# Sampled tokens' expert halves over one and a half passes, their row broadcasts on ScalarE's queue

## The chip, the cores and the metric

The kernel runs on one core of a Trainium2 chip. The time is device microseconds of one execution, first to last instruction with what lies around them. Before the change: median 3320.12 us of three runs (3313.13, 3320.12, 4272.85).

## What is computed

One decoding layer for 256 prompt tokens (with 16 meta tokens ahead) and 32 sampled tokens (8 sequences of 4), all in float32: an input projection, an RWKV-7 mixer and a sparse attention side by side, an output projection, a layer norm, and a retrieval of experts ("PEER"), then the last layer norm. The change concerns the experts:

```python
q = (xf @ wq).reshape(n, PEER_HEADS, 2, PEER_HALF)          # 8 heads
s = jnp.einsum('nhpd,hpkd->nhpk', q, subkeys)               # 2 x 128 keys
# top 16 of each half, top 16 of their sums: 8 x 16 = 128 experts a token, of 128 x 128
h = gelu(einsum('nd,nhkd->nhk', xb, u_tab[eb]))             # row of U against the token
y = einsum('nhk,nhkd->nd', gb * h, v_tab[eb])               # gate * h times row of V
```

U and V have 16,384 rows of 2048 values each.

## The kernel before

**Prompt tokens, all experts.** The 256 prompt tokens (ND) are multiplied by the whole of U and V, and a gate that is zero for experts not chosen does the selecting. `peer_experts` walks a list of 288 weight tiles of 1 MB, `tiles`, each [128, 2048]: 16 "o" (output projection), 16 "q" (queries), with 32 "u" tiles between them, then 32 more "u" of the first half of the experts (half 0), the value pass of half 0 ("v", tiles 96 to 159, `v_zero` = 96), the U pass of half 1 (tiles 160 to 223, `u_one` = 160) and the value pass of half 1 (224 to 287, `v_one` = 224). A value pass is two sweeps of 32 tiles, one for each half of the output columns.

**One tile's way.** SP loads it into one of four buffers once the tile four before it is used. ScalarE rounds it to float32r (`raise_tile`, L2050), waiting for the load and for the tile two before to be used. VectorE subtracts to get the low part (`lower_tile`, L2393). TensorE forms three products of high and low parts (`split_product`, L254 to L256), 48 matmuls a tile. For a "v" tile the gates of two experts are split likewise: ScalarE in L2086, VectorE in L2400. For a "u" tile ScalarE applies Gelu on the way out (`curve`, L2112 and L2116) and VectorE multiplies by gates (`weigh`, L2602). Every engine has one loop over the tiles; in its turn t ScalarE rounds tile t + 2 and VectorE lowers tile t + 2 before the other work of turn t. Each engine works in the order written.

**Gates of half 1.** They are kept in DRAM (`g_rest`), 32 steps of 8 tokens. In the U pass of half 1 Pool reads step k back into one of three buffers `rest` for tile 160 + k; ScalarE (`spread_gates`, L2130) and VectorE (`times`, L2615) use it, and Pool waits for both of step k - 3.

**Sampled tokens, chosen experts only.** For each of the 32 sampled tokens 128 rows of U are gathered, one a partition, in two halves of 1024 columns, so 64 halves n. Buffers `u_row` and `u_x` exist twice. For half n:

- Pool waits for the sum of half n - 2, broadcasts the token's half row from DRAM (`x_rows`) to all partitions of `u_x` (L2014) and gathers the rows with an indirect DMA into `u_row` (L2016), both counted on `u_in`;
- VectorE multiplies them in turn v_zero + n (`times_x`, L2557), after `lower_tile` and `lower_gates` of that turn;
- ScalarE sums along the row in the turn after (`sum_products`, L2134).

So a half is due at every tile of the value pass of half 0. Then the sums are joined (`join_halves`, turn 161), Gelu is applied, and from tile 165 on every second tile TensorE forms one token's value rows (`own_values`, L2274), 32 in all, in bank 7. Pool gathers them (L2027) into `v_row`, two buffers in the same place as `u_row` and `u_x`; the reads of `g_rest` stand between the gathers on its queue. `y_rows` is copied out in turn `v_one` + 5, turned back and added to the sampled tokens' columns, which the second sweep of half 1's values (from tile 256) waits for.

Of the kernel before, what the change touches and what calls it, by code (L numbers as in the profile page):

```python
# [19 lines left out]
P = 128  # L20
# [5 lines left out]
TS = B * S  # L26
# [1754 lines left out]
HALF = D // 2  # L1781
G8 = 8
ND = NY - TS
STEPS = ND // G8
# [52 lines left out]
def peer_experts(cx, a, xT, ident, x_rest, gb, ones, high, low, g_rest, x_rows):  # L1837
# [8 lines left out]
    with ExitStack() as st:  # L1846
# [23 lines left out]
        u_row, u_x = [lay("u_row0", [P, HALF])], [lay("u_x0", [P, HALF])]  # L1870
# [4 lines left out]
        rest = [sb(f"rest{s}", [P, EH, G8]) for s in range(3)]  # L1875
# [35 lines left out]
        for p in pair:  # L1911
# [21 lines left out]
        weighed, g_raised, g_lowered = cx.sem("px_weighed"), cx.sem("px_g_high"), cx.sem("px_g_low")  # L1933
        x_turned, x_taken, x_stored, listed = (cx.sem(f"px_{x}") for x in ("x_turned", "x_taken", "x_stored", "listed"))
        u_in, v_in = ([cx.sem(f"px_{x}{k}") for k in range(2)] for x in ("u_in", "v_in"))
        u_timed, u_summed, u_joined, u_curved, v_ready, v_used = (cx.sem(f"px_{x}") for x in (
            "u_timed", "u_summed", "u_joined", "u_curved", "v_ready", "v_used"))
        y_kept, y_turned, y_added = (cx.sem(f"px_{x}") for x in ("y_kept", "y_turned", "y_added"))
        v_zero, u_one, v_one = tile_of["v", 0, 0, 0], tile_of["u", 1, 0], tile_of["v", 1, 0, 0]
        FIRST_V = 5  # L1940
        finished, drained, link = cx.sem("px_finished"), cx.sem("px_drained"), cx.sem("px_link")

        early = [t for t, x in enumerate(tiles) if x[0] != "v"]
# [14 lines left out]
        def step_number(hf, k):  # L1958
            return hf * STEPS + k
# [6 lines left out]
        with cx.block() as block:  # L1966
# [30 lines left out]
            @block.gpsimd  # L1997
            def _(pool):
                pool.wait_ge(x_taken, 4)
                pool.dma_start(x_rows, xrows).then_inc(x_stored, 16)  # L2000
                for k in range(STEPS):
                    pool.wait_ge(rest_copied, k + 1)
                    pool.dma_start(g_rest[k], rest[k % 3][:].rearrange("p e t -> p (e t)")) \
                        .then_inc(rest_stored[k % 3], 16)

                halves = a["peer_u_rows"].rearrange("e (h d) -> (e h) d", h=2)
                pool.wait_ge(x_stored, 16)
                pool.wait_ge(listed, 3)
                pool.wait_ge(placed, STEPS)
                for n in range(2 * TS):  # L2010
                    if n >= 2:
                        pool.wait_ge(u_summed, n - 1)
                    part_ = x_rows[n // 2:n // 2 + 1, n % 2 * HALF:n % 2 * HALF + HALF]
                    pool.dma_start(u_x[n % 2], bass.AP(part_.tensor, part_.offset, [[0, P], [1, HALF]])) \  # L2014
                        .then_inc(u_in[n % 2], 16)
                    pool.indirect_dma_start(u_row[n % 2], None, halves, bass.IndirectOffsetOnAxis(  # L2016
                        ids[:, 1 + n % 2, n // 2:n // 2 + 1], 0)).then_inc(u_in[n % 2], 16)

                for s in range(3):
                    pool.wait_ge(rest_stored[s], 16 * len(range(s, STEPS, 3)))  # L2020

                def fetch_values(j):
                    if j < 2:
                        pool.wait_ge(u_summed, 2 * TS)
                    else:
                        pool.wait_ge(v_used, j - 1)
                    pool.indirect_dma_start(v_row[j % 2], None, a["peer_v"], bass.IndirectOffsetOnAxis(  # L2027
                        ids[:, 0, j:j + 1], 0)).then_inc(v_in[j % 2], 16)

                for k in range(STEPS):  # L2030
                    if k >= 3:
                        pool.wait_ge(timed, step_number(1, k - 3) + 1)
                        pool.wait_ge(spread, step_number(1, k - 3) + 1)
                    pool.dma_start(rest[k % 3][:].rearrange("p e t -> p (e t)"), g_rest[k]) \
                        .then_inc(rest_loaded[k % 3], 16)
                    if k >= 3 and k % 2:
                        fetch_values((k - 3) // 2)
                for j in range((STEPS - 2) // 2, TS):
                    fetch_values(j)

            def from_pair(k):
# [3 lines left out]
            def _(act):  # L2045
# [73 lines left out]
                def spread_gates(hf, k):  # L2119
# [9 lines left out]
                        src = rest[k % 3][:]  # L2129
                    act.activation(gates[:, n:EH, k * G8:k * G8 + G8], src[:, n:EH, :], ACT.Copy).then_inc(spread, 1)  # L2130

                def sum_products(n):
                    act.wait_ge(u_timed, n + 1)
                    act.activation(u_row[n % 2], u_row[n % 2], ACT.Copy,  # L2134
                                   accum_out=acts[:, n // 2, n % 2:n % 2 + 1]).then_inc(u_summed, 1)

                for k in range(4):
                    raise_x(k)
# [2 lines left out]
                for t, x in enumerate(tiles):  # L2141
                    if x[0] == "o" and t:
                        square_chunk(t - 1)
                    if t == KT - 1:
                        square_chunk(KT - 1)
                    if t + 2 < NT:
                        raise_tile(t + 2)
                        if tiles[t + 2][0] == "v":
                            raise_gates(t + 2)
                    if t == KT - 1:  # L2150
                        root()
                        for k in range(4):
                            bend(k)
                    if x[0] == "q":
                        take_query(t)
                    elif x[0] == "u":
                        curve(t)
                    if t and tiles[t - 1][0] == "q":
                        copy_score(tiles[t - 1][1])
                    head, r = divmod(t + 1 - KT, PER_HEAD)  # L2160
                    if r == 4 and 1 <= head <= PH:
                        act.wait_ge(diffed, head)
                        act.activation(diff[:], diff[:], ACT.Exp).then_inc(exped, 1)
                    for hf, k in after[t]:
                        spread_gates(hf, k)
                    if 0 <= t - 1 - v_zero < 2 * TS:
                        sum_products(t - 1 - v_zero)
                    if t == u_one + 2:
                        act.wait_ge(u_joined, 1)
                        act.activation(own[:], own[:], ACT.Gelu).then_inc(u_curved, 1)  # L2170
                    if t == v_one + 5:
                        act.wait_ge(v_used, TS)
                        act.activation(y_rows, bank[7][:], ACT.Copy).then_inc(y_kept, 1)

            @block.tensor
            def _(pe):
# [107 lines left out]
                for t, x in enumerate(tiles):  # L2284
                    if x[0] == "v":
                        down(t)
                    else:
                        product(t)
                    if t == 1:
                        shift_sum()  # L2290
                    if t == KT - 1:
                        norm_sums()
                    if 1 <= t - KT <= 4:
                        turn_rows(t - KT - 1)
                    j, odd = divmod(t - u_one - FIRST_V, 2)
                    if 0 <= j < TS and not odd:
                        own_values(j)
                    if t == v_one + 6:
                        turn_back()
                    if t and tiles[t - 1][0] == "q":  # L2300
                        score_chunk(tiles[t - 1][1])
                    if t == place_first - 1:
                        turn()
                    for hf, k in after[t]:
                        if hf == 0:
                            place(k)

            @block.vector
            def _(v):
# [243 lines left out]
                    v.tensor_copy(xrows[:, 512 * r:512 * r + 512], bank[7][0:TS, :]).then_inc(x_taken, 1)  # L2553

                def times_x(n):
                    v.wait_ge(u_in[n % 2], 32 * (n // 2 + 1))
                    v.tensor_tensor(u_row[n % 2], u_row[n % 2], u_x[n % 2], ALU.mult).then_inc(u_timed, 1)  # L2557

                def join_halves():
# [7 lines left out]
                def own_column(j):  # L2567
                    if j >= 2:
                        v.wait_ge(v_used, j - 1)
                    v.tensor_scalar(column[j % 2][:], iota[:, 0:TS], float(j), own[:, j:j + 1], ALU.is_equal,  # L2570
                                    ALU.mult).then_inc(v_ready, 1)
# [52 lines left out]
                for t, x in enumerate(tiles):  # L2624
# [21 lines left out]
                        lower_x(3, 1)  # L2646
                    if 1 <= t - KT <= 4:
                        take_rows(t - KT - 1)
                    if 0 <= t - v_zero < 2 * TS:
                        times_x(t - v_zero)  # L2650
                    if t == u_one + 1:
                        join_halves()
                    if t == u_one + 3:
                        spread_own()
                    j, odd = divmod(t + 1 - u_one - FIRST_V, 2)
                    if 0 <= j < TS and not odd:
                        own_column(j)
                    if t == v_one + 7:
                        add_own()
                    if 0 <= t - KT < PER_HEAD * PH + 5:  # L2660
                        select(t - KT)
# [150 lines left out]
```

## Time and profile before

| | us |
|---|---|
| median of three runs | 3320.12 |
| profiled execution | 3312.37 |
| its span, first to last instruction | 3310.7 |
| TensorE busy in the span | 2949.3 (89%) |
| VectorE busy | 1935.5 (58%) |
| ScalarE busy | 1094.9 (33%) |
| Pool busy | 248.4 (8%) |

The profile is that of one execution. "Busy" for TensorE counts overlapped matmuls once. DMA issuing is not counted as busy on an engine; the instruction is shown with the time it held the issuing queue. "Landing" is from a DMA's issue to its last byte. A wait is idle time of an engine just before an instruction, with the instruction or DMA that ended it. The granted clock is a share of TensorE's 2.4 GHz.

### The profile page before, as it was taken

To read this page: it belongs to the slowest core of one execution; us is meant where nothing else is said; L and a number is where in the kernel's file an instruction comes from. 1 tells how busy PE (TensorE), PEld (TensorE's weight loads), DVE (VectorE), ACT (ScalarE), POOL (GpSimd) and SP (SyncE) were. 2 spreads that over 40 slices of the span, in tenths; PEclk is the share of its full clock that TensorE was granted. 3 is DMA by queue.
4 is the path that set the end of the run, shared out by engine and by line. 5 is a ranking of instruction groups with operands and counts; after the bars stand their busy time and mean duration, and the time that the engine had idled before them with its cause. 6 is when DMAs were issued, how large, how long until landed. Compare 5 with 4: busy or idle time off the path is not lost. (4 is left out here: it accounts for less than half of the span.)

```text
span 3310.7 us, 52455 instructions
## 1 busy us (share of the span) xinstructions
PE 2949.3 (89%) x21558; PEld 2652.6 (80%) x21558; DVE 1935.5 (58%) x3399; ACT 1094.9 (33%) x1333; POOL 248.4 (8%) x357
## 2 busy tenths in 40 slices
PE   3999947999985687798999999999999999999995
PEld 2999916878762233497999999999999999999995
DVE  3444336666646763266999989666664444444554
ACT  1222211211112110134444433555554433344441
POOL 0000000000003101100000000232231100000000
PEclk7999957998986557898999999999999999999998
DMA  2444300000015403463555454899998777755551
GB/s 113 152 156 160 112 29 11 17 11 21 11 38 136 153 2 113 146 217 119 182 172 171 168 179 172 307 341 338 332 330 297 286 271 250 253 177 180 182 187 55
DMA packets 145613, 541.86 MB, mean 164 GB/s; under 512 B 25226, under 2 KB 45427, under 8 KB 114387
## 3 DMA queue, kind: packets, MB, share of 16 engines
q1 hardware_dynamic: 110018, 400.11, 35.3%
q0 software_dynamic: 35376, 138.70, 11.9%
q8 instruction: 154, 2.52, 0.3%
q14 instruction: 65, 0.52, 0.0%
HBM read 521.85 MB, written 16.80 MB: 163 GB/s over the span
## 5 line engine op out<-in xcount | busy, mean ns | idle before, releaser
L2393 DVE TENSOR_TENSOR px_w_r<-px_w,px_wh 128x2048 fp32r<-128x2048 f32 x287 | 657.1, 2290 | 461.1 <-ACT px_wh L2050 457.5
L2050 ACT ACTIVATE px_wh<-px_w 128x2048 fp32r<-128x2048 f32 x287 | 549.7, 1915 | 960.6 <-PE px_bank L256 784.9
L254 PE MATMUL px_bank<-pe_high,px_wh 128*128 128x256 f32 (+1 forms) x2560 | 737.1, 288 | 29.2 <-DVE pe_low L2319 14.4
L255 PE MATMUL px_bank<-pe_low,px_wh 128*128 128x256 f32 (+1 forms) x2560 | 733.7, 287 | 0.0
L256 PE MATMUL px_bank<-pe_high,px_w_r 128*128 128x256 f32 (+1 forms) x2560 | 729.3, 285 | 0.0
L254 PEld LDWEIGHTS px_bank<-pe_high,px_wh 128*128 128x128 f32 x2560 | 487.9, 191 | 58.2 <-issue 37.6
L255 PEld LDWEIGHTS px_bank<-pe_low,px_wh 128*128 128x128 f32 x2560 | 486.9, 190 | 0.0
L256 PEld LDWEIGHTS px_bank<-pe_high,px_w_r 128*128 128x128 f32 x2560 | 484.5, 189 | 0.0
L254 PE MATMUL px_pair<-px_arena_gh,px_wh 128*128 128x256 f32 x1024 | 291.5, 285 | 15.5 <-DVE px_arena_gl L2400 15.5
L254 PE MATMUL px_bank<-px_arena_gh,px_wh 128*128 128x256 f32 x1024 | 290.8, 284 | 7.4 <-DVE px_arena_gl L2400 7.2
L255 PE MATMUL px_pair<-px_arena_gl,px_wh 128*128 128x256 f32 x1024 | 290.3, 284 | 0.0
L256 PE MATMUL px_pair<-px_arena_gh,px_w_r 128*128 128x256 f32 x1024 | 290.2, 283 | 0.0
L255 PE MATMUL px_bank<-px_arena_gl,px_wh 128*128 128x256 f32 x1024 | 289.7, 283 | 0.0
L256 PE MATMUL px_bank<-px_arena_gh,px_w_r 128*128 128x256 f32 x1024 | 289.7, 283 | 0.0
L254 PE MATMUL in_acc<-mixT_r,in_wh 128*128 128x304 f32 x784 | 238.4, 304 | 40.5 <-DVE in_w_r L314 40.5
L256 PE MATMUL in_acc<-mixT_r,in_w_r 128*128 128x304 f32 x784 | 238.9, 305 | 0.0
L255 PE MATMUL in_acc<-x_inT_r,in_wh 128*128 128x304 f32 x784 | 237.1, 302 | 0.0
L254 PEld LDWEIGHTS px_pair<-px_arena_gh,px_wh 128*128 128x128 f32 x1024 | 197.1, 192 | 17.9 <-DVE px_w_r L2393 16.9
L254 PEld LDWEIGHTS px_bank<-px_arena_gh,px_wh 128*128 128x128 f32 x1024 | 196.5, 192 | 11.4 <-DVE px_w_r L2393 8.0
L255 PEld LDWEIGHTS px_pair<-px_arena_gl,px_wh 128*128 128x128 f32 x1024 | 197.2, 193 | 0.0
L256 PEld LDWEIGHTS px_pair<-px_arena_gh,px_w_r 128*128 128x128 f32 x1024 | 197.1, 192 | 0.0
L255 PEld LDWEIGHTS px_bank<-px_arena_gl,px_wh 128*128 128x128 f32 x1024 | 196.5, 192 | 0.0
(469 smaller groups left out, 4688.4 us busy)
## 6 DMA issues: line engine op xcount, KB each, us to landing
px_w<-in_peer_u SPq DMA_DIRECT2D x128, 1024.0 KB, 4.9
px_w<-in_peer_v SPq DMA_DIRECT2D x128, 1024.0 KB, 5.8
in_w<-in_w_in SPq DMA_DIRECT2D x49, 1024.0 KB, 4.9
px_w<-in_peer_wq SPq DMA_DIRECT2D x16, 1024.0 KB, 5.0
px_lay_u_x<-x_rows POOLq DMA_DIRECT2D x32, 512.0 KB, 5.9
px_arena_u_x<-x_rows POOLq DMA_DIRECT2D x32, 512.0 KB, 6.0
px_w<-in_w_o SPq DMA_DIRECT2D x15, 1024.0 KB, 5.0
pq_pages<-in_kv_pages SPq DMA_DIRECT2D x48, 256.0 KB, 6.9
```

Of the source, the lines that this page charges most:

```text
L254: pe.matmul(out, w_high, high, start=start, stop=False, skip_group_check=True)
L255: pe.matmul(out, w_high, low, start=False, stop=False, skip_group_check=True)
L256: return pe.matmul(out, w_low, high, start=False, stop=stop, skip_group_check=True)
L2050: act.activation(w_high[t % 2][:], w[t % SL][:], ACT.Copy).then_inc(raised, 1)
L2393: v.tensor_tensor(w_low[t % SL][:], w[t % SL][:], w_high[t % 2][:], ALU.subtract) \
```

## The change

- The 64 halves are no longer due at every tile of one pass. `half_at` gives the tile of each: halves 0 to 47 at tiles 96 + 4n // 3 (96, 97, 98, 100, 101, 102, 104, ...: three of every four tiles), halves 48 to 63 at every second tile from 160 on (160, 162, ... 190).
- The broadcast of the token's half row leaves Pool's queue. ScalarE issues it (`fetch_x`), for half n + 2 right after it has summed half n, and for halves 0 and 1 two tiles ahead of the value pass. It has semaphores of its own, `u_x_in`, and `times_x` waits for both.
- Pool's queue mixes the gathers of halves with the reads of `g_rest`: all reads up to step T - 160 stand before the gather for tile T. The gathers of value rows come after all of them.
- Joining, Gelu and spreading move to tiles 193 to 195. Value rows are used at tiles 198 + 5j // 3 (198, 199, 201, 203, 204, ... 249) instead of every second tile from 165; copying out, turning back and adding move to tiles 250, 251 and 252 (before: 229 to 231).

The diff, cut to its core:

```diff
-        FIRST_V = 5
+        half_at = {v_zero + 4 * n // 3 if n < 48 else u_one + 2 * (n - 48): n for n in range(2 * TS)}
+        joined_at = u_one + 33
+        value_at = {joined_at + 5 + 5 * j // 3: j for j in range(TS)}
+        kept_at = max(value_at) + 1
...
-                for n in range(2 * TS):
+                def fetch_half(n):
                     if n >= 2:
                         pool.wait_ge(u_summed, n - 1)
-                    part_ = x_rows[n // 2:n // 2 + 1, n % 2 * HALF:n % 2 * HALF + HALF]
-                    pool.dma_start(u_x[n % 2], bass.AP(part_.tensor, part_.offset, [[0, P], [1, HALF]])) \
-                        .then_inc(u_in[n % 2], 16)
                     pool.indirect_dma_start(u_row[n % 2], None, halves, bass.IndirectOffsetOnAxis(
                         ids[:, 1 + n % 2, n // 2:n // 2 + 1], 0)).then_inc(u_in[n % 2], 16)
...
+                def fetch_rest(k):
+                    if k >= 3:
+                        pool.wait_ge(timed, step_number(1, k - 3) + 1)
+                        pool.wait_ge(spread, step_number(1, k - 3) + 1)
+                    else:
+                        pool.wait_ge(rest_stored[k], 16 * len(range(k, STEPS, 3)))
+                    pool.dma_start(rest[k % 3][:].rearrange("p e t -> p (e t)"), g_rest[k]) \
+                        .then_inc(rest_loaded[k % 3], 16)
...
+                k = 0
+                for t, n in half_at.items():
+                    while k < STEPS and k <= t - u_one:
+                        fetch_rest(k)
+                        k += 1
+                    fetch_half(n)
+                for k in range(k, STEPS):
+                    fetch_rest(k)
+                for j in range(TS):
                     fetch_values(j)
...
+                def fetch_x(n):
+                    part_ = x_rows[n // 2:n // 2 + 1, n % 2 * HALF:n % 2 * HALF + HALF]
+                    act.dma_start(u_x[n % 2], bass.AP(part_.tensor, part_.offset, [[0, P], [1, HALF]])) \
+                        .then_inc(u_x_in[n % 2], 16)
+
                 def sum_products(n):
                     act.wait_ge(u_timed, n + 1)
                     act.activation(u_row[n % 2], u_row[n % 2], ACT.Copy,
                                    accum_out=acts[:, n // 2, n % 2:n % 2 + 1]).then_inc(u_summed, 1)
+                    if n + 2 < 2 * TS:
+                        fetch_x(n + 2)
...
+                    if t == v_zero - 2:
+                        act.wait_ge(x_stored, 16)
+                        act.wait_ge(placed, STEPS)
+                        fetch_x(0)
+                        fetch_x(1)
+                    if t - 1 in half_at:
+                        sum_products(half_at[t - 1])
...
                 def times_x(n):
-                    v.wait_ge(u_in[n % 2], 32 * (n // 2 + 1))
+                    v.wait_ge(u_in[n % 2], 16 * (n // 2 + 1))
+                    v.wait_ge(u_x_in[n % 2], 16 * (n // 2 + 1))
...
-                    if 0 <= t - v_zero < 2 * TS:
-                        times_x(t - v_zero)
-                    if t == u_one + 1:
+                    if t in half_at:
+                        times_x(half_at[t])
+                    if t == joined_at:
                         join_halves()
```

## Rows read from the trace of the kernel before

**Rows 1.** Stretches: length, busy us of PE, PEld, DVE, ACT, POOL; clock, DMA share, GB/s.
```profile
2080.00:2480.00 400.00, 377.12 (x3092) 373.19 (x3091) 261.14 (x201) 224.40 (x254) 109.37 (x124) 1.00 0.92 333
2480.00:2513.00 33.00, 30.19 (x243) 29.99 (x242) 16.42 (x21) 15.28 (x21) 5.77 (x9) 0.95 0.81 296
2513.00:2700.00 187.00, 187.00 (x1547) 172.35 (x1546) 83.56 (x106) 78.33 (x116) 28.97 (x41) 1.00 0.79 289
2935.00:3240.00 305.00, 305.00 (x2544) 305.00 (x2544) 156.74 (x118) 129.16 (x106) 0.00 (x0) 1.00 0.56 183
```

**Rows 2.** Instructions on the weight tiles, 2940 to 3240 us: durations, first and last start.
```profile
L2393 DVE TENSOR_TENSOR px_w_r<-px_w,px_wh x52: 2291/2292/2293, 2943.0 to 3236.8; 128x2048 fp32r<-128x2048 f32 x52
...
DMA to landing us min/median/max: 4.9/5.0/6.3
```

**Rows 3.** The same view, 2079 to 2500 us.
```profile
L2393 DVE TENSOR_TENSOR px_w_r<-px_w,px_wh x68: 2277/2285/2294, 2079.9 to 2499.4; 128x2048 fp32r<-128x2048 f32 x68
L1993 SPq DMA_DIRECT2D px_w<-in_peer_v x61: 367/368/368, 2083.6 to 2455.7; - x61
...
DMA to landing us min/median/max: 5.0/8.3/10.8
```

**Rows 4.** TensorE's waits, 2080 to 2494 us: us in total, times, longest.
```profile
PE px_pair L254 <- DVE px_arena_gl L2400: 15.5, 13, 2.3
PE px_bank L254 <- DVE px_arena_gl L2400: 7.2, 7, 1.6
PE px_bank L254 <- DVE px_w_r L2393: 2.8, 1, 2.8
```

**Rows 5.** VectorE's waits in the same stretch.
```profile
DVE px_lay_u_row L2557 <- DMA px_lay_u_row<-in_peer_u_rows,px_ids: 68.5, 22, 5.6
DVE px_arena_u_row L2557 <- DMA px_arena_u_row<-in_peer_u_rows,px_ids: 50.5, 20, 4.8
```

**Rows 6.** Timeline (start us, us) of one unstalled tile, last value pass: ScalarE, VectorE, TensorE.
```profile
2998.69 1.92 ACT L2050 ACTIVATE px_wh<-px_w 128x2048 fp32r<-128x2048 f32 x1 [3.32 <-PE px_bank L256]
3000.51 0.61 ACT L2086 ACTIVATE px_arena_gh<-px_gates 128x512 fp32r<-128x512 f32 x1
...
3000.64 2.29 DVE L2393 TENSOR_TENSOR px_w_r<-px_w,px_wh 128x2048 fp32r<-128x2048 f32 x1 [2.87 <-ACT px_wh L2050]
3002.85 0.68 DVE L2400 TENSOR_TENSOR px_arena_gl<-px_gates,px_arena_gh 128x512 fp32r<-128x512 f32 x1
...
3004.19 0.28 PE L254 MATMUL px_bank<-px_arena_gh,px_wh 128*128 128x256 f32 x1
```

**Rows 7.** Timeline of one half in the first value pass: VectorE, ScalarE, Pool.
```profile
2347.06 0.68 DVE L2400 TENSOR_TENSOR px_arena_gl<-px_gates,px_arena_gh 128x512 fp32r<-128x512 f32 x1
2347.66 1.22 DVE L2557 TENSOR_TENSOR px_arena_u_row<-px_arena_u_row,px_arena_u_x 128x1024 f32<-128x1024 f32 x1
...
2348.91 1.06 ACT L2134 ACTIVATE px_arena_u_row<-px_arena_u_row 128x1024 f32<-128x1024 f32 x1
...
2350.36 0.54 POOL L2014 DMA_DIRECT2D px_arena_u_x<-x_rows  x1 [1.76 <-ACT px_arena_u_row L2134]
2351.20 1.33 POOL L2016 DMA_INDIRECT px_arena_u_row<-in_peer_u_rows,px_ids  x1 [0.30 <-issue]
```

**Rows 8.** Landings: the second of `u_row`'s buffers, then the value rows.
```profile
DMA to landing us min/median/max: 5.7/8.4/10.8
...
DMA to landing us min/median/max: 6.0/7.2/8.0
```

**Rows 9.** SP's reads of the bias rows: issue durations ns, and one with its landing.
```profile
L1119 SPq DMA_DIRECT2D ay_bias<-bias_rows x3: 434/1870/4581, 1061.2 to 1063.6; - x3
...
ay_bias<-bias_rows SPq DMA_DIRECT2D x1, 1024.0 KB, 6.6
```

**Rows 10.** VectorE and ScalarE, 2494 to 2906 us: busy, mean ns, idle before.
```profile
L2393 DVE TENSOR_TENSOR px_w_r<-px_w,px_wh 128x2048 fp32r<-128x2048 f32 x65 | 149.0, 2292 | 229.7 <-ACT px_wh L2050 229.7
...
L2050 ACT ACTIVATE px_wh<-px_w 128x2048 fp32r<-128x2048 f32 x66 | 126.3, 1914 | 254.6 <-PE px_bank L256 254.6
```

More of the change, by code:

```diff
@@ L1935, in peer_experts @@
         u_in, v_in = ([cx.sem(f"px_{x}{k}") for k in range(2)] for x in ("u_in", "v_in"))
+        u_x_in = [cx.sem(f"px_u_x_in{k}") for k in range(2)]
         u_timed, u_summed, u_joined, u_curved, v_ready, v_used = (cx.sem(f"px_{x}") for x in (
@@ L2009, in _ @@
                 pool.wait_ge(placed, STEPS)
-                for n in range(2 * TS):
+                def fetch_half(n):
                     if n >= 2:
                         pool.wait_ge(u_summed, n - 1)
-                    part_ = x_rows[n // 2:n // 2 + 1, n % 2 * HALF:n % 2 * HALF + HALF]
-                    pool.dma_start(u_x[n % 2], bass.AP(part_.tensor, part_.offset, [[0, P], [1, HALF]])) \
-                        .then_inc(u_in[n % 2], 16)
                     pool.indirect_dma_start(u_row[n % 2], None, halves, bass.IndirectOffsetOnAxis(
                         ids[:, 1 + n % 2, n // 2:n // 2 + 1], 0)).then_inc(u_in[n % 2], 16)
-                for s in range(3):
-                    pool.wait_ge(rest_stored[s], 16 * len(range(s, STEPS, 3)))
+                def fetch_rest(k):
[6 more added lines that the diff above has]
+                        .then_inc(rest_loaded[k % 3], 16)
                 def fetch_values(j):
@@ L2028, in fetch_values @@
                         ids[:, 0, j:j + 1], 0)).then_inc(v_in[j % 2], 16)
[L2030 to L2038, printed above, removed]
+                k = 0
[7 more added lines that the diff above has]
+                for j in range(TS):
                     fetch_values(j)
@@ L2165, in _ @@
                         spread_gates(hf, k)
-                    if 0 <= t - 1 - v_zero < 2 * TS:
-                        sum_products(t - 1 - v_zero)
-                    if t == u_one + 2:
+                    if t == v_zero - 2:
[5 more added lines that the diff above has]
+                        sum_products(half_at[t - 1])
+                    if t == joined_at + 1:
                         act.wait_ge(u_joined, 1)
                         act.activation(own[:], own[:], ACT.Gelu).then_inc(u_curved, 1)
-                    if t == v_one + 5:
+                    if t == kept_at:
                         act.wait_ge(v_used, TS)
@@ L2294, in _ @@
                         turn_rows(t - KT - 1)
[L2295 to L2298, printed above, removed]
+                    if t in value_at:
+                        own_values(value_at[t])
+                    if t == kept_at + 1:
                         turn_back()
@@ L2648, in _ @@
                         take_rows(t - KT - 1)
-                    if 0 <= t - v_zero < 2 * TS:
-                        times_x(t - v_zero)
-                    if t == u_one + 1:
+                    if t in half_at:
+                        times_x(half_at[t])
+                    if t == joined_at:
                         join_halves()
-                    if t == u_one + 3:
+                    if t == joined_at + 2:
                         spread_own()
[L2655 to L2658, printed above, removed]
+                    if t + 1 in value_at:
+                        own_column(value_at[t + 1])
+                    if t == kept_at + 2:
                         add_own()
```

## The prediction

> **What bounds the kernel now.** The page's first part comes first: TensorE is by far the busiest engine, so the question is where the change's stretch leaves it idle. The busy time by stretch answers that [rows 1]. The sampled tokens' halves run in the first value pass, about 2080 to 2480 us. There TensorE is busy 377.12 of 400 us and the DMA engines are 92% busy at 333 GB/s. The second U pass (2513 to 2700) and the undisturbed part of the last value pass (2935 to 3240) have TensorE busy all the time, with DMA at 79% and 56%. Only the first value pass and the 33 us after it (30.19 busy, granted clock 0.95 of the 2.4 GHz level) have something to give back.
>
> How much is read from the pace of the weight tiles, one VectorE subtraction (L2393) each. In the last value pass 52 of them start between 2943.0 and 3236.8 us: 293.8 / 51 = 5.76 us for a tile without a stall [rows 2]. From 2079.9 to 2499.4 there are 68, so 67 steps in 419.5 us [rows 3]. Unstalled they would take 67 x 5.76 = 385.9 us. **33.6 us** is therefore all that can come back. The table of waits names 25.5 us of it: TensorE waits for the low half of the gates 15.5 + 7.2 us and for a lowered tile 2.8 us, both made by VectorE [rows 4]. The other 8 us, refilling after each gap and the lower clock, I do not split; it goes with the gaps.
>
> VectorE is late because `times_x` stands in its order ahead of the next `lower_tile` and waits for its row DMA: 68.5 + 50.5 us in 42 waits, 2.8 us each [rows 5].
>
> **The round trip that decides.** Let R be the start of a tile's rounding on ScalarE (L2050). Without a stall, from the last value pass [rows 6]: R = 2998.69; VectorE's subtraction starts at R + 1.95, its gate subtraction at R + 4.16; the next tile's matmuls start at 3004.19 = R + 5.50 and the next R is 5.76 later. The gates are low at 3002.85 + 0.68 = R + 4.84, which leaves 0.6 us before TensorE would notice. In the first value pass `times_x` follows 0.60 us after the start of the gate subtraction and takes 1.22 us [rows 7], so on time it runs from R + 4.76 to R + 5.98. VectorE's next subtraction starts at R + 5.76 + 1.95 = R + 7.71, so 1.7 us are spare. A half may come 1.7 + 0.6 = 2.3 us after VectorE asks before TensorE stops.
>
> The same buffer's next half: ScalarE sums after the following tile's rounding and gates, at R + 5.76 + 1.82 + 0.61 = R + 8.19. Pool acts 1.45 us after the sum's start, first with the broadcast of x, and 0.84 us later with the indirect row (2350.36 and 2351.20 against 2348.91 [rows 7]): R + 10.48. It lands a median 8.4 us later, at most 10.8 [rows 8]. VectorE asks two tiles on, at R + 11.52 + 4.76 = R + 16.28. So the kernel before affords a landing of 16.28 + 2.3 - 10.48 = 8.1 us and gets 8.4. That is why it keeps losing a little.
>
> **The change, part by part.**
>
> *Broadcast off Pool's queue.* Pool loses 0.84 us ahead of each indirect row (64 times), so the row starts at R + 9.64 and may take 8.9 us. At the median 8.4 it comes 9.64 + 8.4 - 16.28 = 1.8 us after VectorE asks: no stall.
>
> *Spreading.* Of each three halves in the value pass (48 in 64 tiles) two get a buffer distance of three tiles and one keeps two. With three tiles the affordable landing is 8.9 + 5.76 = 14.7 us, above the worst landing of 10.8. Only the 16 with two tiles are near the limit. The bytes of halves per tile fall by a quarter. The near bound for the landing is that of the value rows in the U pass, 7.2 us for twice the bytes at 79% DMA [rows 8, 1], the far one 10.8. I take 8.4, nothing improved, and no stall; for single late ones I put 2 us. The bounds are 0 and 16 x (10.8 - 8.9) = 30 us.
>
> *The broadcast on ScalarE.* No row shows ScalarE issuing a DMA. The nearest are SP's: 0.37 us for a tile of weights [rows 3], 0.43 to 4.58 us for SP's three reads of the bias rows, which overlap in DRAM and are cut into sixteen short runs a partition [rows 9]. I take 0.4, because one run of 4 KB for each of 128 partitions is far nearer to a tile of value weights (two such runs). It hides in ScalarE's 3.32 us idle per value tile [rows 6], of which the sum takes at most 1.45: 1.9 stay. What queues behind it is the next rounding, and VectorE and TensorE behind that; with the cover gone each microsecond costs up to 64 us. The broadcast lands between 5.0 us (a weight tile) and 6.6 us (1 MB of bias rows) [rows 2, 9], before the row with its 8.4. `fetch_x(0)` and `fetch_x(1)` wait, two tiles before the pass, for placements that TensorE finished before the rounding ahead of them, so for nothing.
>
> *Halves and gate reads in the U pass.* Sixteen halves come every second tile at a distance of three to four tiles. VectorE idles 229.7 us before 65 subtractions there and ScalarE 254.6 before 66 roundings [rows 10], 3.5 and 3.9 us each, against 1.22 for the product and 1.85 for sum and issue in every second one. Without that cover: 16 x 3 = 48 us. On Pool's queue each of these rows now stands behind reads of `g_rest` that wait for steps three tiles earlier. Three tiles are 17 us and the worst landing is 10.8, so the row is still there in time. The first reads are issued earlier than before, not later.
>
> *Values later.* Their 32 groups of matmuls move from tiles 165 to 227 to 198 to 249 and cost TensorE the same. The distance of a buffer falls from four tiles to three, 17 us against 7.2 us landing plus about 1 of issue. The turn back is done by tile 252; the last half pass asks for it at 256.
>
> *The added semaphore* on `times_x` waits for a transfer that is there first: nothing.
>
> *A third queue.* The weights land in 5.0 us when SP's queue runs alone and in 8.3 (at most 10.8) beside Pool's [rows 2, 3]; they are asked for two tiles, 11.5 us, after issue. I expect no stall, since the bytes only fall. The Trainium skill, page "DMA: Bandwidth & Descriptors", section "Queues, rings and completion order", speaks against it: each DMA engine serves in turn the queue rows that have work, so one more row takes a share from SP's. By it the rival "weights late" below would be the outcome; the slowdown of 3.3 us beside one other queue agrees with it, and no run here yet shows three.
>
> **Sum.** The profiled execution took 3312.4 us. 3312.4 - 33.6 + 2 = **3281 us**. The three runs are 3313, 3320 and 4273; the lower two set the level, 3320 is 8 us above the profiled one, and the forecast is for undisturbed runs.
>
> **Rivals.**
>
> 1. *The halves stay late.* At 92% DMA busy the landing, not the issue, sets the pace, and the 16 short distances all see 10.8 us: 30 us stay, 3309. For it: the landing is 8.4 where the same engines at 79% give 7.2 for twice the bytes. Against: a quarter fewer half bytes, and 48 of 64 halves get 5.8 us or more of slack.
> 2. *Weights late* by the third queue. If a second rival queue adds as much as the first, 3.3 us, weights land between 11.6 and 14.1 us, 0.1 to 2.6 us late; the middle, 1.3 us, on the 48 tiles with a half gives 65 us: 3344. It decides when the landing exceeds 11.5 + 0.6 us. Against: total bytes fall.
> 3. *ScalarE blocked by its issue* (the other side). An issue over 1.9 + 0.6 = 2.5 us makes every rounding behind it late. At 4.58 us each, 64 x 2.1 = 133 us: 3414. For it only the bias rows with their many runs; against it the weights' 0.37 us.
>
> **How the numbers follow.** The forecast 0.76, rival 1 0.12, rival 2 0.05, rival 3 0.04, and 0.03 for what I do not see. The likeliest one's own range is 3274 (all 33.6 back and 5 us below) to 3296 (half the bound of 30, or runs 8 us above the profile). With rival 1 the range is 3274 to 3314. A measurement of this kernel tells about 2% (66 us) from no change. The stretch holds only 33.6 us, so faster by that much is 0.01; slower needs rival 3, or rival 2 at its worst: 0.04; within it 0.95.
>
> **What would show it.** Right: steps of 5.76 us in the first value pass, no waits of TensorE for L2400 or L2393 there, clock 1.00 around its end, VectorE's waits for the rows under 2.3 us and at every third half only, weights landing at 8 us or less, ScalarE's issues near 0.4 us. Wrong: ScalarE rounding late behind its own issue, ScalarE waiting for weights instead of TensorE, row landings above 8.9 us, or a new wait for Pool's rows in the U pass.

## The result, and the profile after

The changed kernel takes a median of 3281.51 us over four runs (3278.67 to 3286.3), against 3316.62 us for the kernel before beside it: a ratio of 0.99, 95% interval 0.9881 to 0.9919. One of the four runs of the kernel before, 4272.85 us, was a slow one and is left out of the ratio. The profiled execution took 3278.67 us against 3312.37, which is 33.7 us less; its span is 3276.9 us against 3310.7.

Busy time by stretch, with the columns of [rows 1]: the first value pass, the part of the second U pass that now holds halves, and the rest of it.

```profile
2083.00:2452.00 369.00, 368.84 (x3074) 368.67 (x3073) 241.81 (x185) 204.42 (x222) 63.51 (x48) 1.00 0.88 317
2452.00:2640.00 188.00, 188.00 (x1583) 188.00 (x1582) 109.29 (x121) 104.40 (x162) 33.73 (x48) 1.00 0.87 318
2640.00:2836.00 196.00, 196.00 (x1625) 180.80 (x1623) 84.95 (x82) 68.70 (x65) 15.52 (x17) 1.00 0.72 258
```

TensorE is busy 368.84 of 369 us where it was 377.12 of 400 [rows 1], and the clock stays at 1.00 through the end of the pass, where it had been 0.95.

The pace, from the instructions on the weight tiles in the first value pass (durations in ns, first and last start; then the loads' landing) [rows 3]:

```profile
L2412 DVE TENSOR_TENSOR px_w_r<-px_w,px_wh x64: 2280/2291/2293, 2085.7 to 2449.0; 128x2048 fp32r<-128x2048 f32 x64
...
DMA to landing us min/median/max: 5.1/7.1/8.9
```

64 subtractions make 63 steps in 2449.0 - 2085.7 = 363.3 us, 5.77 us each: the unstalled pace of [rows 2] to 0.01 us. The weights land in 7.1 us, earlier than before.

TensorE's waits from 2083 us on, all that is left of [rows 4]:

```profile
PE px_pair L254 <- DVE px_arena_gl L2419: 0.2, 1, 0.2
```

VectorE's waits from 2083 to 2640 us [rows 5]:

```profile
DVE px_w_r L2412 <- ACT px_wh L2058: 205.9, 95, 3.3
```

There is one kind of wait, for the rounding, and none for a row DMA: the 119.0 us of [rows 5] are gone altogether. The rows land earlier too [rows 8], in the two buffers in turn:

```profile
DMA to landing us min/median/max: 4.6/5.9/8.6
...
DMA to landing us min/median/max: 4.7/5.6/8.0
```

One half in the first value pass, VectorE's product and then ScalarE and its DMA queue ("ACTq"), as in [rows 7]:

```profile
2336.57 1.22 DVE L2577 TENSOR_TENSOR px_lay_u_row<-px_lay_u_row,px_lay_u_x 128x1024 f32<-128x1024 f32 x1
...
2337.57 1.92 ACT L2058 ACTIVATE px_wh<-px_w 128x2048 fp32r<-128x2048 f32 x1 [2.29 <-PE px_pair L256]
2337.83 0.33 ACTq L2142 DMA_DIRECT2D px_lay_u_x<-x_rows  x1
2339.39 0.61 ACT L2094 ACTIVATE px_arena_gh<-px_gates 128x512 fp32r<-128x512 f32 x1
2339.91 1.04 ACT L2147 ACTIVATE px_lay_u_row<-px_lay_u_row 128x1024 f32<-128x1024 f32 x1
...
2341.31 1.31 POOL L2018 DMA_INDIRECT px_lay_u_row<-in_peer_u_rows,px_ids  x1 [4.45 <-ACT px_lay_u_row L2147]
```

The broadcast of the next half goes out at 2337.83 us. The product that frees its buffer ended at 2336.57 + 1.22 = 2337.79. In the program the issue stands behind the sum, yet it leaves 2.1 us before the sum starts (2339.91), while the rounding still runs. The row leaves Pool at 2341.31, when the broadcast is already 3.5 us under way. In the kernel before the two stood 0.84 us apart on one queue.

### The profile page after: what moved, and what is told of

It reads as the page before. It is cut to its first block and busy times, and to the rows that moved or that the text cites. A ratio compares the mean times of both kernels' runs of the same rounds, so it can differ in the third digit from the quotient of the medians.

```text
span 3276.9 us, 52521 instructions
## 1 busy us (share of the span) xinstructions
PE 2937.4 (90%) x21558; PEld 2646.6 (81%) x21558; DVE 1935.6 (59%) x3399; ACT 1090.7 (33%) x1333; POOL 217.8 (7%) x293
```

## Experiments

The theory at the outset was that of the prediction: the round trip of a half's buffer (sum, issue, landing, product) against two tile times decides, and both parts of the change relax it. It held besides that the load on the DMA engines, 92% busy, lengthens the landing, so that fewer bytes help; that is what the prediction's rival 1 rests on too. The rival here was the queue: on Pool's queue a row waits behind its own broadcast.

### Each part alone

**Spreading alone.** The new schedule, with the broadcast back on Pool's queue ahead of its row.

```diff
 (against the changed kernel)
                     if n >= 2:
                         pool.wait_ge(u_summed, n - 1)
+                    pool.dma_start(u_x[n % 2], ...).then_inc(u_x_in[n % 2], 16)
                     pool.indirect_dma_start(u_row[n % 2], ...)
...
-                    if n + 2 < 2 * TS:
-                        fetch_x(n + 2)
...
```

> The halves at the new tiles, the broadcasts still issued by Pool ahead of each row. My theory (a round trip against a limit, lengthened by the load on the DMA engines): with a quarter fewer half bytes per tile the rows land in 7 to 8 us against the limit of 8.1 at the 16 short distances, so nearly all comes back: 3279 to 3286 us, VectorE's waits for rows at every third half only, under 2.3 us. Rival (the queue decides, since a row waits behind its own broadcast on Pool's queue): rows land at 8.4 us or more as before, the 16 short distances lose 0.3 to 2.5 us each: 3284 to 3318 us.

3282.83 us, 0.9901 (0.9885 to 0.9918): the whole gain within the noise. VectorE's waits for rows, and the one wait of TensorE:

```profile
DVE px_lay_u_row L2568 <- DMA px_lay_u_row<-in_peer_u_rows,px_ids: 9.5, 7, 2.2
DVE px_arena_u_row L2568 <- DMA px_arena_u_row<-in_peer_u_rows,px_ids: 7.9, 4, 3.8
...
PE px_bank L254 <- DVE px_w_r L2403: 2.8, 1, 2.8
```

VectorE waits 11 times instead of 42, and TensorE notices once, at the end of the pass. The longest wait, 3.8 us, is above the 2.3 us that I had expected at most. The rows land in 7.8 and 8.0 us, hardly sooner than before.

**ScalarE's queue alone.** The schedule of before, with the broadcasts issued by ScalarE.

```diff
 (against the kernel before)
-                    pool.dma_start(u_x[n % 2], ...).then_inc(u_in[n % 2], 16)
...
                                    accum_out=acts[:, n // 2, n % 2:n % 2 + 1]).then_inc(u_summed, 1)
+                    if n + 2 < 2 * TS:
+                        fetch_x(n + 2)
```

> A half at every tile as before, only the broadcasts moved to ScalarE's queue. My theory: the bytes stay at 2.1 MB a tile, which at the 333 GB/s of the stretch before takes 6.3 us, more than the 5.76 of a tile, so rows land late again: 3297 to 3313 us, DMA engines 92% busy or more. Rival (the queue decides): rows land in 5.5 to 6 us as in the changed kernel, well inside the limit of 8.9: 3279 to 3284 us.

3280.76 us, 0.9889 (0.9873 to 0.9906): the whole gain again. My expectation, 3297 to 3313 us because of the bytes, missed; the time is the rival's. First value pass by busy time, and the rows' landings:

```profile
2084.00:2452.00 368.00, 367.77 (x3063) 367.43 (x3063) 258.45 (x201) 219.21 (x251) 81.34 (x61) 1.00 0.97 359
```

```profile
DMA to landing us min/median/max: 4.5/6.1/8.8
...
DMA to landing us min/median/max: 4.8/6.2/9.3
```

It moves the bytes of before in less time, 359 GB/s with the DMA engines 97% busy, and TensorE doesn't stall. So 92% at 333 GB/s [rows 1] was no ceiling of the DMA engines, and the part of the theory that rests on their load falls, the prediction's rival 1 with it. Whether it was the queue, the next section tests.

**No broadcasts.** The kernel before leaving out the broadcasts of halves 2 to 63, so that the sampled tokens' output is not the layer's.

```diff
 (against the kernel before)
-                    pool.dma_start(u_x[n % 2], ...).then_inc(u_in[n % 2], 16)
+                    if n < 2:
+                        pool.dma_start(u_x[n % 2], ...).then_inc(u_in[n % 2], 16)
```

> The kernel before with the broadcasts of halves 2 to 63 left out (every product uses the first token's row, so the sampled tokens' output is not the layer's). It takes 32 of 64 MB off the stretch and 0.84 us off Pool ahead of each row. Both theories: no stall, 3278 to 3284 us. Beside e2 it tells bytes from the queue: if e2 stays late and this does not, the bytes did it.

3278.25 us, 0.9882 (0.9865 to 0.9898). The rows land in 4.8 us. Even with the broadcasts' transfers gone the time is that of the changed kernel, so there was no more to gain from the broadcasts.

**SP's queue.** The changed kernel with the broadcasts on the queue of the weights: two queues instead of three.

```diff
 (against the changed kernel)
+                    if t - 5 in half_at and half_at[t - 5] + 2 < 2 * TS:
+                        sp.wait_ge(u_timed, half_at[t - 5] + 1)
+                        fetch_x(half_at[t - 5] + 2)
...
-                    if n + 2 < 2 * TS:
-                        fetch_x(n + 2)
```

> The changed kernel with the broadcasts issued on SP's queue, behind the weight load of five tiles on, at about the same time as ScalarE issues them. So two queues carry what three carry in the changed kernel. My theory: the same time, 3278 to 3287 us, since all lands inside its limits. A rival by the number of queues: weights land sooner than the 7.1 us of the changed kernel, near 5 to 6, and rows later than 5.8, near 7; if rows pass 8.9 the time rises by up to 16 x 1.9 = 30 us, to 3310.

3277.47 us, 0.9883 (0.9867 to 0.99). The weights land in 6.6 us (median) instead of 7.1, and ScalarE waited for them in neither kernel. The rows land in 6.3 and 6.1 us, and VectorE waits for one of them, 0.6 us. The third queue is not what the gain rests on.

### Is it the queue or the moment?

| rows' landing, medians of the two buffers, us | half at every tile | spread |
|---|---|---|
| broadcast just ahead of the row, on Pool | 8.2 and 8.4 (before) | 7.8 and 8.0 |
| broadcast on ScalarE, after the product | 6.1 and 6.2 | 5.9 and 5.6 (after) |

Spreading, with its fewer bytes a tile, took 0.2 to 0.6 us off, moving the broadcast 1.9 to 2.4 us. Two runs separate the queue from the moment.

**Early, on Pool's own queue.**

```diff
 (against the kernel before)
                     if n >= 2:
-                        pool.wait_ge(u_summed, n - 1)
+                        pool.wait_ge(u_timed, n - 1)
                     pool.dma_start(u_x[n % 2], ...)
+                    if n >= 2:
+                        pool.wait_ge(u_summed, n - 1)
                     pool.indirect_dma_start(u_row[n % 2], ...)
```

> The kernel before (a half at every tile, all on Pool's queue), but Pool issues a half's broadcast as soon as the product of two halves earlier is done, and only then waits for the sum and issues the row. So the broadcast leaves some 3 us sooner, on the same queue. Theory WHEN (the move to ScalarE helps because its issue needs the product alone and leaves early): as with the broadcasts on ScalarE, 3278 to 3285 us, rows landing in about 6 us. Theory WHERE (a row waits behind its own broadcast as long as both are on one queue): rows still land at 8 us, the time between 3290 and 3315.

3281.19 us, 0.9892 (0.9856 to 0.9929). Pool's timeline and the landings:

```profile
2341.43 0.54 POOL L2014 DMA_DIRECT2D px_arena_u_x<-x_rows  x1 [1.36 <-DVE px_arena_u_row L2559]
2344.48 1.35 POOL L2018 DMA_INDIRECT px_arena_u_row<-in_peer_u_rows,px_ids  x1 [2.51 <-ACT px_arena_u_row L2136]
```

```profile
DMA to landing us min/median/max: 5.1/6.2/10.7
...
DMA to landing us min/median/max: 5.2/6.5/10.3
```

The broadcast leaves 3.05 us ahead of the row, and one changed wait on the old queue gives the gain within the noise. (The value pass still takes 372.4 us, by the first matmul on tiles 96 and 160, where the changed kernel takes 369.0.)

**Late, on ScalarE's queue.** ScalarE alone, with a wait for the sum ahead of the issue.

```diff
 (against "ScalarE's queue alone")
                     if n + 2 < 2 * TS:
+                        act.wait_ge(u_summed, n + 1)
                         fetch_x(n + 2)
```

> A half at every tile, broadcasts on ScalarE's queue, but ScalarE waits for its own sum before it issues, so the broadcast leaves at about the time Pool issues the row. Theory WHEN: rows land near 8 us again and VectorE waits 1 to 2 us for most halves, just inside the limit of 2.3 or a little over: 3282 to 3300. Theory WHERE: rows land at 6 us or so, few waits, 3279 to 3284.

3284.07 us, 0.9904 (0.9868 to 0.9939). One half (sum, broadcast, row), the landings, and VectorE's waits:

```profile
2344.71 1.04 ACT L2137 ACTIVATE px_lay_u_row<-px_lay_u_row 128x1024 f32<-128x1024 f32 x1
...
2345.87 0.33 ACTq L2132 DMA_DIRECT2D px_lay_u_x<-x_rows  x1
...
2346.11 1.31 POOL L2014 DMA_INDIRECT px_lay_u_row<-in_peer_u_rows,px_ids  x1 [4.45 <-ACT px_lay_u_row L2137]
```

```profile
DMA to landing us min/median/max: 4.6/7.9/10.6
...
DMA to landing us min/median/max: 5.7/7.8/9.4
```

```profile
DVE px_lay_u_row L2569 <- DMA px_lay_u_row<-in_peer_u_rows,px_ids: 37.5, 27, 3.8
DVE px_arena_u_row L2569 <- DMA px_arena_u_row<-in_peer_u_rows,px_ids: 19.7, 21, 1.9
```

The broadcast leaves 0.24 us ahead of the row. With a queue of its own, but late, it holds the rows back again: 7.8 and 7.9 us. So the moment sets the landing; the queue can account for 0.3 to 0.6 us at most (8.2 and 8.4 before). The time is still close to the changed kernel's: the row leaves 0.84 us earlier than before and lands some 0.4 us sooner, so VectorE waits (37.5 + 19.7) / 48 = 1.2 us on a late half, which is below the 2.3 us at which TensorE notices; the longest, 3.8 us, is above, and TensorE waits 2.2 us in all.

### What the spreading is worth

Each part alone suffices, so the other is margin. To see it, the round trip was made longer: Pool issues tiny loads (32 bytes each, to an unused buffer `spare`) ahead of each row, eight or three of them.

```diff
+        spare = sb("spare", [P, 32])
...
                     if n >= 2:
                         pool.wait_ge(u_summed, n - 1)
+                        for i in range(8 * n, 8 * n + 8):        # or 3 * n, 3 * n + 3
+                            pool.dma_start(spare[i % P:i % P + 1, 8 * (i // P):8 * (i // P) + 8],
+                                           x_rows[0:1, 0:8]).then_inc(spared, 16)
```

Eight, on the kernel with ScalarE's queue alone:

> A half at every tile, broadcasts on ScalarE's queue, and ahead of each row Pool issues eight tiny loads into a spare tile (0.55 us each by its reads of the gates, 4.4 us together, almost no bytes). The limit of 8.9 us from the round trip is then used as 4.4 + 6.2 = 10.6, 1.7 us over at every half: between half and the whole of that on 62 halves, 53 to 105 us more: 3333 to 3386. If the limit were not what decides, about 3281.

Eight, on the changed kernel:

> The changed kernel with the same eight tiny loads ahead of each row. Only the 16 halves at a distance of two tiles should be over the limit, by 4.4 + 5.8 - 8.9 = 1.3 us, so 21 us more: 3290 to 3306. The difference to the run with a half at every tile is what the spreading is worth when the round trip is too long. If the spreading gave no slack, as slow as that run.

Three, on the kernel with ScalarE's queue alone:

> A half at every tile, broadcasts on ScalarE's queue, three tiny loads by Pool ahead of each row instead of eight (1.5 us). The limit of 8.9 us is then used as 1.5 + 6.2 = 7.7: waits of VectorE near 9.64 + 7.7 - 16.28 = 1.1 us on most halves, all inside the 2.3 that cost nothing: 3279 to 3288. If every wait of VectorE cost TensorE its length, 62 x 1.1 = 68 us more: 3349.

Three, on the changed kernel:

> The changed kernel with the same three tiny loads ahead of each row: no half over the limit and Pool not full (some 3 to 4 us a half against 5.76): 3279 to 3285. With eight loads Pool's own queue held 5.4 to 7 us a half; if it was that, and not the spreading giving no slack, this run shows nothing lost.

| tiny loads | every tile | spread | difference |
|---|---|---|---|
| eight | 3361.47 us, 1.0137 (1.01 to 1.0174) | 3343.53, 1.0092 (1.0062 to 1.0123) | 18 us |
| three | 3325.22, 1.003 (1.0017 to 1.0042) | 3310.33, 0.9993 (0.998 to 1.0006) | 15 us |

The first, eight loads at every tile, came as expected. VectorE's waits there, first value pass:

```profile
DVE px_lay_u_row L2573 <- DMA px_lay_u_row<-in_peer_u_rows,px_ids: 101.4, 26, 9.9
DVE px_arena_u_row L2573 <- DMA px_arena_u_row<-in_peer_u_rows,px_ids: 87.4, 27, 7.4
```

By the prediction's account the row comes 9.64 + 4.4 (eight loads) + 6.2 - 16.28 = 4.0 us after VectorE asks; measured (101.4 + 87.4) / 53 = 3.6.

The other three missed. In both spread kernels TensorE loses time mainly at every fourth tile (100, 104, 108, ...), behind the halves that keep two tiles, as the account says; with eight loads the tile after most of these loses another 1.5 us. But the price is too high, and Pool's timeline shows that the tiny loads aren't a plain delay. With eight, spread:

```profile
2097.00 4.05 POOL L2021 DMA_DIRECT2D px_spare<-x_rows  x8 [21.94 <-ACT px_lay_u_row L2152]
2101.35 2.68 POOL L2023 DMA_INDIRECT px_lay_u_row<-in_peer_u_rows,px_ids  x1 [0.30 <-issue]
2104.02 4.00 POOL L2021 DMA_DIRECT2D px_spare<-x_rows  x8
```

The row's issue holds Pool 2.68 us where it took 1.31 in the changed kernel, and the next half's loads begin right behind it: 7.0 us of Pool's queue for this half, while two of every three halves are followed by the next one a tile, 5.76 us, later. With three loads, every tile, the landing itself rose; VectorE's waits (2084 to 2460 us), and the landings of the first of `u_row`'s buffers, then the second:

```profile
DVE px_arena_u_row L2573 <- DMA px_arena_u_row<-in_peer_u_rows,px_ids: 109.1, 25, 5.9
...
DVE px_lay_u_row L2573 <- DMA px_lay_u_row<-in_peer_u_rows,px_ids: 19.2, 8, 4.8
```

```profile
DMA to landing us min/median/max: 4.6/6.5/9.6
...
DMA to landing us min/median/max: 5.0/8.2/9.7
```

Most of the waiting is at the buffer whose rows land in 8.2 us: 9.64 + 1.85 (three loads) + 8.2 - 16.28 = 3.4 us after VectorE asks, above 2.3, against 109.1 / 25 = 4.4 measured. At 6.2 us it would have been 1.4, below it, which is what I had expected. With three loads, spread, the rows land in 7.2 and 7.1 us, and the account is short again: 9.64 + 1.85 + 7.1 - 16.28 = 2.3 us late, against (29.7 + 27.6) / 16 = 3.6 measured. Why the rows land later behind a few tiny loads, and why both runs with three are some 1 us beyond the sum, stays open. The worth of the spreading, 15 to 18 us once the round trip is too long, holds for delays of this kind. All four kernels share the unused buffer `spare`, which makes the last pass some 4 us shorter (see the last section), so it drops out of the differences.

### How long may ScalarE issue?

The prediction allows ScalarE's issue 2.5 us, since it puts the issue behind the sum. The profile after shows it leaving earlier. To tell the accounts apart, ScalarE issues 12 or 24 tiny loads behind each broadcast in the changed kernel.

```diff
 (against the changed kernel)
+        spare = sb("spare", [P, 48])        # 24 loads: [P, 96]
...
                         fetch_x(n + 2)
+                        for i in range(12 * n, 12 * n + 12):        # or 24 * n, 24 * n + 24
+                            act.dma_start(spare[i % P:i % P + 1, 8 * (i // P):8 * (i // P) + 8],
+                                          x_rows[0:1, 0:8]).then_inc(spared, 16)
```

> The changed kernel with twelve tiny loads issued by ScalarE after each broadcast, 12 x 0.33 = 4.0 us of issuing at each half. By the account on record (an issue of over 2.5 us delays the next rounding) 4.3 - 2.5 = 1.8 us late, on 48 halves 86 us more, 3360 or so, a little less if part of it overlaps. By what the trace of the changed kernel shows (ScalarE's queue issues while its earlier activations still run, right after the product) the issue may take from R + 6 to the next rounding at R + 11.5, 5.4 us: no loss, 3279 to 3285.

> The same with twenty-four, 24 x 0.33 + 0.33 = 8.3 us at each half. By the account on record 5.8 us late each, 48 x 5.8 = 278 us or more. If ScalarE's queue issues ahead of its activations, 8.3 - 5.4 - 0.6 = 2.3 us late, 48 x 2.3 = 110 us more and somewhat more by the clock: 3370 to 3420.

Twelve: 3254.55 us, 0.9816 (0.9798 to 0.9834). ScalarE and its queue:

```profile
2344.76 0.34 ACTq L2144 DMA_DIRECT2D px_arena_u_x<-x_rows  x1
...
2346.37 2.40 ACTq L2154 DMA_DIRECT2D px_spare<-x_rows  x8
2349.53 1.92 ACT L2060 ACTIVATE px_wh<-px_w 128x2048 fp32r<-128x2048 f32 x1 [3.21 <-PE px_pair L256]
```

The broadcast and twelve loads hold the queue from 2344.76 to 2348.77 us, 4.0 us (4.4 for the next half). They end 0.8 us before the next rounding, which waits for TensorE, as it should. Over the 62 halves the issuing takes 4.0 to 4.9 us. At six of them the rounding starts 0.1 us behind the last issue, as it does with twenty-four loads below, so it was held there or nearly so; TensorE waits 3.8 us in all. So twelve loads cost little, and are close to the limit. Twenty-four: 3422.73 us, 1.0321 (1.0302 to 1.0341), just above the 3370 to 3420 us of the second account and far below the first's.

```profile
2338.17 0.34 ACTq L2144 DMA_DIRECT2D px_lay_u_x<-x_rows  x1
...
2339.26 6.73 ACTq L2154 DMA_DIRECT2D px_spare<-x_rows  x22
2346.10 1.92 ACT L2060 ACTIVATE px_wh<-px_w 128x2048 fp32r<-128x2048 f32 x1 [6.79 <-issue]
```

Here the rounding starts when the issues end ("issue"), 7.9 us after the first of them, and VectorE and TensorE are late behind it: 141 us over the changed kernel. Issuing takes 7.7 to 8.6 us a half, and the rounding waits for it every time. So rival 3's mechanism exists, but its threshold lies near the 4.0 to 4.9 us of the twelve, not at 2.5.

The run with twelve is also the fastest kernel of all, 27 us below the changed one, which no account had foreseen; the last section takes it up.

## Why the prediction was right

**The ceiling** carried it, and was right for this change: 33.6 us predicted, 33.7 measured in the profiled executions. By the first matmul on tiles 96, 160 and 224 and the end, the first value pass became shorter by 397.9 - 369.0 = 28.9 us and the second U pass by 404.8 - 383.9 = 20.9, while the last pass became longer by 388.2 - 371.7 = 16.5: 14 tokens' value matmuls moved there from the U pass, at 1.18 us each. The balance is 33.3. The 4.4 us that the U pass gains beyond the move are its two late first tiles before (8.7 and 7.2 us where the changed kernel takes 5.7), which the 67 steps of the ceiling include.

**The round trip** was right as an account. The row of before comes 10.48 + 8.4 - 16.28 = 2.6 us after VectorE asks, and [rows 5] has 2.8; "late, on ScalarE's queue" gives 9.64 + 7.9 - 16.28 = 1.3 and has 1.2; with eight tiny loads it is 4.0 and 3.6. These three agree to 0.4 us; with three tiny loads it is 1 us short (3.4 against 4.4).

**The landing was mis-sized.** "I take 8.4, nothing improved" is the term that failed; it is 5.6 and 5.9. The forecast did not suffer because it called for no stall already at 8.4. I had counted the broadcast as an instruction that leaves Pool, 0.84 us, and not as 512 KB that travel beside the row. The broadcast needs only the product, the row needs the sum; sent after the product, it is well under way when the row leaves. The Trainium skill, page "DMA: Bandwidth & Descriptors", section "Issuing engines are not separate DMA queues", says that issuing from several engines saves only the sequencer's time of issuing. By it the gain would be Pool's 0.84 us, with the landing unchanged; the runs agree that the queue matters little (early on Pool's queue 6.2 and 6.5 us, late on ScalarE's 7.8 and 7.9), but the move to a second engine also brought an earlier issue, worth 1.9 to 2.4 us of landing.

**VectorE's waits** were expected under 2.3 us at every third half. There are none. The row leaves at R + 9.64 and VectorE asks at R + 16.28, so a short distance grants 6.6 us before VectorE waits at all; the sixteen rows with a short distance landed in 5.0 to 5.9 us. The slowest of all, 8.6 us, was one in the U pass, where the distance is four tiles.

**ScalarE's issue** took 0.33 us for 0.4 predicted, but its place was wrong. The prediction has it behind the sum, with 1.9 us of cover; it leaves with the product, 2.1 us before the sum, and 4.0 to 4.9 us of issuing cost TensorE only 3.8 us of waits in all. The error made rival 3 too likely, not the forecast wrong.

**The parts don't add.** The working credits the broadcast with 0.84 us and the spreading with 5.8 us of slack, and the sum of both with 33.6 us. Each alone gives all of it, since the round trip was only just too long. I had not said so.

**Rival 1** rested on 92% busy DMA engines as a limit. They reached 97% and 359 GB/s without a stall of TensorE. The landing was late because the broadcast travelled with the row.

**Rival 2** did not come: the weights land in 7.1 us with three queues and 8.3 with two before [rows 3]. Two more runs bear on the rule of the Trainium skill (page "DMA: Bandwidth & Descriptors", section "Queues, rings and completion order") that the prediction cites for it, that a DMA engine serves in turn the queue rows that have work. The weights land in 8.3 us with three queues at before's bytes (ScalarE's queue alone), and in 6.6 with two at the changed kernel's (SP's queue). The third queue cost 0.5 us of landing at most, far from the 3.3 feared, and the loads are asked for 11.5 us after issue.

**The 2 us for single late halves** were not needed: the profiled execution took 3278.67 us for a sum of 3281. The median of the runs is 2.8 us above the profiled one, as before's was 4.3 above its own. That it meets the sum to 0.5 us is therefore luck: the sum is for a profiled execution, and was 2.3 us too high there.

## What to carry to other kernels

When a loop loses a few per cent to a transfer that is just late, write the buffer's round trip as a sum against the time that the loop grants, and read from the trace what the late transfer travels with: whatever depends on less than it should be sent earlier, on whichever queue can wait for the right thing. Here one changed wait on Pool gave the same 1% as a new schedule and a new queue. Two cures for one limit don't add; what the second is worth shows only when the round trip is made longer.

## What the hardware showed that was not expected

**A DMA issued by ScalarE leaves ahead of activations that stand before it in the program**, once the waits ahead of it are met: at 2337.83 us against a sum that began at 2339.91. Only a wait on the sum itself held it ("late, on ScalarE's queue"). The description ahead of the prediction, that each engine works in the order written, does not hold for such an issue.

**TensorE's pace in the value pass moved with an unused buffer.** `spare` was put ahead of the buffers of the split gates and of others, which moves them by 128 bytes a partition with 32 columns, 192 with 48 and 384 with 96. The last value pass has no halves and no tiny loads, and the clock is 1.00. The same stretch of 170 us there, with the columns of [rows 1]: the changed kernel,

```profile
3045.00:3215.00 170.00, 170.00 (x1419) 170.00 (x1419) 84.14 (x59) 72.48 (x59) 0.00 (x0) 1.00 0.53 174
```

three tiny loads, every tile (128 bytes),

```profile
3060.00:3230.00 170.00, 170.00 (x1435) 170.00 (x1434) 89.29 (x68) 73.03 (x60) 0.00 (x0) 1.00 0.57 186
```

and twelve loads on ScalarE (192 bytes).

```profile
3020.00:3190.00 170.00, 170.00 (x1465) 169.89 (x1464) 90.77 (x70) 73.66 (x61) 0.00 (x0) 1.00 0.56 182
```

TensorE is busy throughout in all three, yet at 48 matmuls a tile a value tile takes 170 x 48 / 1419 = 5.75 us, 5.69 and 5.57. With 384 bytes it is 5.69 again. By the first matmuls of the tiles, all eight kernels without `spare` go at 5.76 us in the second sweep of that pass, and all four with 32 columns at 5.69 to 5.70. Tiles of the U pass, which don't read these buffers, keep 5.70 (1348 matmuls in 160 us after; 1012 in 120 us with 192 bytes). The kernel with twelve loads gains 8.7 us in the first value pass (369.0 to 360.3) and 15.1 in the last (388.2 to 373.1): 23.8 of the 23.9 us between the two profiled executions. So the "unstalled" 5.76 us that served as the ceiling is no floor of TensorE.

But the layout cannot be all of it. VectorE's subtractions in the last pass of the kernel with twelve loads, early and late, then in the U pass of "spreading alone" and of the changed kernel, which have the same layout:

```profile
L2418 DVE TENSOR_TENSOR px_w_r<-px_w,px_wh x11: 2284/2293/2293, 3018.5 to 3072.9; 128x2048 fp32r<-128x2048 f32 x11
...
L2418 DVE TENSOR_TENSOR px_w_r<-px_w,px_wh x19: 2292/2293/2294, 3089.6 to 3191.4; 128x2048 fp32r<-128x2048 f32 x19
...
L2403 DVE TENSOR_TENSOR px_w_r<-px_w,px_wh x29: 2291/2292/2293, 2476.8 to 2635.1; 128x2048 fp32r<-128x2048 f32 x29
...
L2412 DVE TENSOR_TENSOR px_w_r<-px_w,px_wh x29: 2291/2293/2294, 2477.6 to 2637.3; 128x2048 fp32r<-128x2048 f32 x29
```

The first two are 54.4 / 10 = 5.44 us a tile and 101.8 / 18 = 5.66, in one pass of one kernel (the 5.57 above is their mix); the last two are 158.3 / 28 = 5.65 and 159.7 / 28 = 5.70 at one layout. So the place of the gates is argued as one cause, since the pace in the last pass differs by the width of `spare`; the loads and their semaphore come with it, and a shift of 192 bytes without the loads was not run. What else selects the pace, and by which mechanism, stays open. The kernel with twelve loads, 0.9816, is the fastest of all runs; its loads compute nothing.
